# The gate of the state-space mixer: after all token tiles, or tile by tile

## The reference

```
h    = rms_norm(x) ;  proj = h @ w_in            # all three mixers' inputs
A    = sparse attention, B = band attention      # 512 columns each
C    = state-space mixer                         # 1024 columns: 16 heads in 4 groups
x   += concat[A, B, C] @ w_out
x   += relu(rms_norm(x) @ w_up)^2 @ w_down
```

```
y = y + d_skip * xs
g = (y * silu(z)).reshape(b, t, 4, 256)
g = g * rsqrt(mean(g * g, axis=-1) + EPS)        # per token and group
out = g.reshape(b, t, 1024) * gate_norm
```

## Time and profile before

| what | value |
|---|---|
| median of three runs | 3196.65 us |
| the profiled execution | 3198.03 us |
| its span, first to last instruction | 3196.3 us |
| TensorE busy | 3107.2 us, 97% |
| VectorE busy | 1714.7 us, 54% |
| ScalarE busy | 1146.5 us, 36% |
| mean granted TensorE clock | 0.982 |
| rate of all transfers | 139 GB/s over the span |

### The profile page before, as it was taken

How to read it: one execution, slowest core, us unless ns; L and a number is a source line. 1 busy time by engine, 2 the same in 40 slices (tenths; PEclk the granted TensorE clock), 3 DMA queues, 4 the chain that set the end, 5 groups by cost and what they waited for, 6 DMA issues and landing times.

```text
span 3196.3 us, 52626 instructions
## 1 busy us (share of the span) xinstructions
PE 3107.2 (97%) x20829; PEld 3054.1 (96%) x20829; DVE 1714.7 (54%) x2135; ACT 1146.5 (36%) x1373; POOL 136.9 (4%) x115
## 2 busy tenths in 40 slices
PE   6999999899999999999999999998999999999998
PEld 5899999799999999999999999987999999999998
DVE  5574467685435444444555735587654444444444
ACT  3334443243333333233323435433433333332333
POOL 4000000020000000000110000000100000000001
PEclk8999999899999999999999999998999999999999
DMA  6444444244445445454444544422454444544542
GB/s 203 122 139 130 148 139 126 66 125 145 149 148 150 150 147 150 151 147 149 151 124 133 155 140 127 146 94 79 145 151 148 148 151 149 147 150 151 147 148 92
DMA packets 233862, 444.41 MB, mean 139 GB/s; under 512 B 23073, under 2 KB 23521, under 8 KB 233425
## 3 DMA queue, kind: packets, MB, share of 16 engines
q1 hardware_dynamic: 228320, 426.37, 44.2%
q0 software_dynamic: 5424, 16.43, 1.6%
HBM read 430.94 MB, written 12.85 MB: 139 GB/s over the span
## 4 chain that ended last, share of the span: by engine, by line
PE 67%; issue 28%; DVE 2%; DVEq 1%; ACT 1%; POOLq 1%; DMA 0%; ACTq 0%; SPq 0%
PE G L682 21%; PE G L683 20%; PE G L684 20%; PE M L719 1%; PE M L957 1%; PE M L851 1%; PE M L905 1%; POOLq L528 1%; PE M L959 0%; DVEq L1375 0%; PE M L796 0%; PE M L777 0%; DMA U<-in_x_prompt 0%; PE M L710 0%; PE M L963 0%
## 5 line engine op out<-in xcount | busy, mean ns | idle before, releaser
L1347 DVE TENSOR_TENSOR raw_parts<-raw,whi 128x1024 fp32r<-128x1024 f32 (+1 forms) x816 | 1016.5, 1261 | 867.0 <-ACT whi L1078 851.4
L1078 ACT ACTIVATE whi<-raw 128x1024 fp32r<-128x1024 f32 (+1 forms) x816 | 849.8, 1045 | 1425.0 <-PE G L684 1389.9
L682 PE MATMUL G<-X_parts,whi 128*128 128x320 f32 x3840 | 1199.7, 312 | 24.8 <-DVE raw_parts L1347 23.3
L684 PE MATMUL G<-X_parts,raw_parts 128*128 128x320 f32 x3840 | 1188.9, 310 | 0.0
L683 PE MATMUL G<-X_parts,whi 128*128 128x320 f32 x3840 | 1188.6, 310 | 0.0
L682 PE MATMUL G<-U_parts,whi 128*128 128x320 f32 x2560 | 798.4, 312 | 12.3 <-DVE U_parts L1516 12.3
L683 PE MATMUL G<-U_parts,whi 128*128 128x320 f32 x2560 | 793.8, 310 | 0.0
L684 PE MATMUL G<-U_parts,raw_parts 128*128 128x320 f32 x2560 | 793.8, 310 | 0.0
L682 PEld LDWEIGHTS G<-X_parts,whi 128*128 128x128 f32 x3840 | 723.2, 188 | 30.8 <-issue 24.8
L683 PEld LDWEIGHTS G<-X_parts,whi 128*128 128x128 f32 x3840 | 723.3, 188 | 0.4
L684 PEld LDWEIGHTS G<-X_parts,raw_parts 128*128 128x128 f32 x3840 | 722.8, 188 | 0.0
(11 more groups left out here) (269 smaller groups left out, 1354.7 us busy)
## 6 DMA issues: line engine op xcount, KB each, us to landing
raw<-in_w_up SPq DMA_DIRECT2D x256, 512.0 KB, 3.7
raw<-in_w_down SPq DMA_DIRECT2D x256, 512.0 KB, 3.7
raw<-in_w_in SPq DMA_DIRECT2D x224, 512.0 KB, 3.6
raw<-in_w_out SPq DMA_DIRECT2D x64, 512.0 KB, 3.7
U<-in_x_prompt SPq DMA_DIRECT2D x2, 1024.0 KB, 7.6
out_y_prompt<-U SPq DMA_DIRECT2D x8, 256.0 KB, 2.5
bias_ext<-XC POOLq DMA_DIRECT2D x2, 768.0 KB, 5.7
raw<-in_w_in SPq DMA_DIRECT2D x16, 80.0 KB, 2.0
```

Source lines behind the costliest of these rows:

```text
L682: pe.matmul(out, hi, xh, start=(i == 0 and k == 0), stop=False)
L684: mm = pe.matmul(out, lo, xh, start=False, stop=(c == part[1] - 1 and k == KC - 1))
L1078: act.activation(whi[:, c % 4, :, cols], raw[:, c, :, cols], ACT.Copy).then_inc(high_done.sem, 1)
L1347: dve.tensor_tensor(wlo[:, c, :, cols], raw[:, c, :, cols], whi[:, c % 4, :, cols].bitcast(F32), ALU.subtract)\
```

## The change

The gate's work is done by tile of tokens and not by group of columns. The squares of tile t (one instruction over all eight blocks) come on ScalarE after the exponents in group (t+1,0); the sums (`gate_sums`, two matmuls of 4 x n columns, all four groups of columns in one bank) on TensorE after `st` of group (t+1,1); the root on ScalarE in that same group; the reciprocal, its application and the split of the operand on VectorE after `weights` in group (t+1,2). The last tile's follow directly on group (2,3). `x_mix` is raised twice, at the end of the last tile. The list of fillings gets three keys `gs` in place of four, two of them between the groups. The due slot of the gate goes.

```diff
@@ mixer_fills
         keys += [("y", t, g), ("st", t, g)]
+        if t and g == 1:
+            keys.append(("gs", t - 1))
         if g < C_GROUPS - 1:
             continue
+        if t == 2:
+            keys.append(("gs", 2))
...
-    keys += [("gs", g) for g in range(C_GROUPS)]
@@ tensor
+                def gate_sums(t):
+                    o, n = TILES[t]
+                    pe.wait_ge(gsq.sem, gsq.at(l, t + 1))
+                    key = ("gs", t)
+                    free_bank(pe, l, key)
+                    for b in range(2):
+                        mm = pe.matmul(mb(key)[:, 0:C_GROUPS * n].rearrange("p (g t) -> p g t", g=C_GROUPS), ones[:],
+                                       SQZ[:, b:2 * C_GROUPS:2, o:o + n], start=(b == 0), stop=(b == 1))
+                    done_filling(mm, key)
...
+                    if t and g == 1:
+                        gate_sums(t - 1)
                     if g < C_GROUPS - 1:
                         continue
+                    if t == 2:
+                        gate_sums(2)
@@ scalar
+                def gate_squares(t):
+                    o, n = TILES[t]
+                    act.wait_ge(gz.sem, gz.at(l, t + 1))
+                    act.activation(SQZ[:, :, o:o + n], Z[:, :, o:o + n], ACT.Square).then_inc(gsq.sem, 1)
+                def gate_roots(t):
+                    o, n = TILES[t]
+                    key = ("gs", t)
+                    filled(act, l, key)
+                    drained(act.activation(GRMS[:, :, o:o + n], mb(key)[:, 0:C_GROUPS * n].rearrange("p (g t) -> p g t", g=C_GROUPS),
+                                           ACT.Sqrt, scale=1.0 / (C_WIDTH // C_GROUPS), bias=eps[:, 0:1]), key)
+                    act.drain().then_inc(grms.sem, 1)
...
+                    if t and g == 0:
+                        gate_squares(t - 1)
+                    if t and g == 1:
+                        gate_roots(t - 1)
                     if g < C_GROUPS - 1:
                         continue
+                    if t == 2:
+                        gate_squares(2)
+                        gate_roots(2)
@@ vector
+                def gate(t):
+                    o, n = TILES[t]
+                    dve.wait_ge(grms.sem, grms.at(l, t + 1))
+                    dve.reciprocal(GRMS[:, :, o:o + n], GRMS[:, :, o:o + n])
+                    dve.drain()
+                    for kb in range(2 * C_GROUPS):
+                        zb = Z[:, kb, o:o + n]
+                        dve.scalar_tensor_tensor(out=zb, in0=zb, scalar=pcol("gate", kb), in1=GRMS[:, kb // 2, o:o + n],
+                                                 op0=ALU.mult, op1=ALU.mult)
+                    dve.drain()
+                    for j in range(2, 4):
+                        m4 = MIX[:, 4 * j:4 * j + 4, o:o + n]
+                        hi, lo = (U_parts[:, i, 4 * j:4 * j + 4, o:o + n] for i in range(2))
+                        dve.tensor_copy(hi, m4)
+                        dve.drain()
+                        ins = dve.tensor_tensor(lo, m4, hi.bitcast(F32), ALU.subtract)
+                        if t == 2:
+                            ins.then_inc(x_mix.sem, 1)
...
                     gated(t, g)                      # raises gz after g == 3
                     if k + 1 < len(groups):
                         weights(*groups[k + 1])
+                    if t and g == 2:
+                        gate(t - 1)
...
-                dve.drain().then_inc(gz.sem, 1)
-                yield due["gate"]
-                gate()
+                gate(2)
```

More of the change, by code:

```diff
@@ L128, in schedule @@
         due["so", t] = at + 5 * t + 5
-    due["gate"] = at + 17
     return due
@@ L408, in trunk @@
     so_out = Count(nc, "state_rows_stored", 2, step=16)
-    gz = Count(nc, "gated", 1)
-    gsq = Count(nc, "gate_squares", 4)
-    grms = Count(nc, "gate_rms", 4)
+    gz = Count(nc, "gated", 3)
+    gsq = Count(nc, "gate_squares", 3)
+    grms = Count(nc, "gate_rms", 3)
     passed = sem("waits_passed")
@@ L1747, in gated @@
                     dve.tensor_tensor(Z[:, 2 * g:2 * g + 2, o:o + n], Z[:, 2 * g:2 * g + 2, o:o + n], YT[:, :, 0:n], ALU.mult)
+                    if g == C_GROUPS - 1:
+                        dve.drain().then_inc(gz.sem, 1)
                     key = ("st", t, g)
@@ L1758, in gated @@
                     dve.drain().then_inc(st_ready.sem, 1)
[L1760 to L1764, removed]
-                        dve.drain()
[L1766 to L1772, removed]
+                def gate(t):
[12 more added lines that the diff above has]
+                        dve.tensor_copy(hi, m4)
+                        dve.drain()
+                        ins = dve.tensor_tensor(lo, m4, hi.bitcast(F32), ALU.subtract)
+                        if t == 2:
+                            ins.then_inc(x_mix.sem, 1)
                 yield due["cb"]
```

## The result

The changed kernel takes 3241.2 us (median of 4 runs, 3240.0 to 3242.3) against 3194.5 us (3190.2 to 3198.3) for the kernel before on the same chip: ratio 1.0152, 95% interval 1.0139 to 1.0164. It is slower by 46.7 us, where 36 were forecast; 3241.2 lies inside the range of 3210 to 3248. The profiled executions differ by 43.3 us (spans of 3239.6 and 3196.3 us).

What follows compares the result with a forecast made beforehand. TensorE, busy 97% of the span, was taken as the bound. Terms 6.9 + 8.7 + 5.4 - 3.0 = 18.0 us per layer, 36.0 for two, took the profiled 3198.03 to 3234.0 us, stated as 3232.7; range 3210 to 3248.

Steps and rivals of the forecast that it cites:

- step 1: Sums of tile 0 on TensorE wait for VectorE to drain their bank: pause, sums and low clock, 6.9 us per layer.
- step 2: VectorE's gate of tile 0 delays the residual, so TensorE stalls at slot 132: 7.3 us plus 1.4 of clock, 8.7.
- step 3: Sums of tile 1, in tile 2, meet the same bank wait: 5.6 us, of which 5.4 arrive at weights of (2,3).
- step 4: Tail after group (2,3): less gate remains, but tile 1's gate stands before `gated` (2,3); 3.0 us gained per layer.
- The clock: After TensorE pauses the following matmuls run at a low clock: 1.7, 1.4 and 1.4 us, 4.5 per layer.
- A: Neither sums nor gate hold TensorE up; only the tail's 3.0 us gain per layer remains, 3190.6 us; chance 3%.
- B: Bank wait not felt; only the gate of tile 0 stalls the unit, 8.1 us per layer, 3212.9 us; chance 7%.
- C: Bank waits as worked out, but the residual of unit 2 not late: 9.3 us per layer, 3215.3 us; chance 6%.
- D: Each new TensorE pause costs 2.8 us of low clock: 3.9 us more per layer, 3240.5 us; chance 15%.

Runs made afterwards that it cites:

- late_sums: Changed kernel with TensorE's sums and ScalarE's root of tiles 0 and 1 moved from group (t,1) to (t,2), one group later; 3221.9 us, ratio 1.0082.
- gates_last: Changed kernel with VectorE's gate of tiles 0 and 1 moved behind the gated product of group (2,3), ahead of tile 2's; 3232.7 us, ratio 1.0120.
- gate_first_table_clear2: gate_first plus a one-column root preloading ScalarE's table, and GpSimd's clearing (not its store) moved behind the split of the last half; 3182.0 us, ratio 0.9963.
- busy_pauses: Changed kernel with TensorE's pauses ahead of the sums of tiles 0 and 1 filled by 6 and 4 zero matmuls; 3225.4 us, ratio 1.0094.
- two_roots_out: Changed kernel with the square roots of tiles 0 and 1 replaced by a copy, so two table switches per layer instead of six; 3243.3 us, ratio 1.0156.
- late_and_last: Changed kernel with the moves of late_sums and gates_last together; 3223.9 us, ratio 1.0088.
- gate_first_clear2: gate_first with GpSimd's clearing of its sums moved behind the split of the last half, the store left in place; 3190.0 us, ratio 0.9979.
- gate_first: Kernel before with the gated product's semaphore raised right behind the product of (2,3) and TensorE's and ScalarE's gate work ahead of the state rows; 3190.2 us, ratio 0.9990.

## Why the prediction was right, and where its size was off

**The pause ahead of the first sums (step 1).** 3.5 us forecast, 3.44 measured, ended by L1706 as named; the delay of what follows 6.9 and 7.06. Shown by late_sums, where the wait is gone.

**The gate of tile 0 (step 2).** 8.1 us of VectorE forecast, 7.9 measured; the stall at slot 132 7.3 and 6.88; slot 132 late by 14.2 us by the sum (6.9 + 7.3) and by the trace. Shown by gates_last, where the stall is gone.

**The second sums (step 3).** Pause 2.5 and 2.57 us. The delay added from slot 132's chunk to (2,2) was put at 5.4 us; the products of (2,2) come at 639.67 where 618.57 less 2.94, 615.63, would be the undelayed start. That is a delay of 24.0 us, and 16.9 had arrived at the products of (2,1) (625.24, before 611.27): 7.1 us.

**The tail (step 4).** 3.0 us of gain forecast; the delay falls from 24.0 to 21.4, 2.7 us. That the gate of tile 1 would stand in front of `gated` (2,3) is seen at 655.27. On its way are the 0.8 us that the 1.09 us cast lost beside GpSimd's clearing, while its fellow takes 0.29. And gate_first_table_clear2 shows that such a gain needs no tiles: the order of the end gives more of it.

**The clock: the term that was mis-sized.** Steps 1 and 2 counted 1.7 and 1.4 us of low clock, step 3 another 1.4, the tail nothing: 4.5 us per layer. Measured in the first layer are 1.9 (7.06 less 3.44 and 1.72 us for the sums), 2.7 (16.9 less 14.2), 2.8 (7.1 less 2.57 and 1.72) and, after the tail, 20 matmuls of 0.47 us instead of 10, some 1.2: about 8.5 us. That is 4 us more per layer, and 18.0 + 4 = 22.

The traces give 22.6 us for the first layer (21.4 and the 1.2) and 23.5 for the second (22.5 and 8 more matmuls at the low level, 1.0), 46.1 us in all. The two profiled executions differ by 43.3, because the changed kernel came to the stage 2.94 us earlier.

What failed was the size of the clock's terms, in three places. Step 2 read half a chunk where nearly a whole one ran at the low level (21 matmuls of 0.47 us after 600.44). Step 3 counted its sums at the full level; they took 3.75 us, and 1.95 in busy_pauses. The tail was given nothing. busy_pauses is the test of it: with the first and the third pause as long but busy, 7.6 us per layer are gone, though the filling accounts directly for 4.5 of them.

**Rivals.** A, B and C needed one of the three waits to be missing; all are there. D, given 15%, came nearest: its price was 8.4 us of low clock per layer and 3240.5 us. Part of that is luck. It put 2.8 us on each of three pauses, measured are 1.9, 2.7 and 2.8, and the 1.2 us behind the tail, which it did not have, fill the gap. No cost of the table switches shows (two_roots_out).

**How the savings combine.** late_sums and gates_last together bring 17.3 of 27.8 us. The waits of late_sums are shorter by only 12.0 + 2.9 + 1.6 - 8.7 = 7.8 of its 19.3 us. The rest is clock. In the first layer's traces it is at the sums, which now take 1.96 and 1.88 us instead of 3.46 and 3.75, and behind the stall at slot 132 (9 matmuls of 0.47 us instead of 21). What gates_last gains is clock behind the same stall, so the two kernels save in part the same thing: against late_sums, late_and_last has waits that are 5.0 us longer for the two layers, and behind slot 132 only 9 slow matmuls per layer are left for it to save. This is read from the traces; no run tests it by itself.

## What to carry to other kernels

Work that is meant to fill an engine's idle time must not stand in the queue in front of something the busiest engine will wait for, and every instruction put on that busiest engine brings its place in the ring of banks with it: ask who drains the bank four keys back. Price a pause of a few microseconds at its length plus two or three microseconds of lower clock (1.9, 2.7 and 2.8 here, and once nothing). Before cutting a tail into pieces, try its order: raising one semaphore earlier, taking the gate ahead of the rows to be stored, preloading the table and keeping GpSimd off the cast gave 8 us here by the trace (7 to 16 by the interval), where the tiles as they were placed cost 47.

## What the runs showed of the hardware

A cast of VectorE from one buffer to another does not run beside GpSimd's clearing. Three casts of 128x1280, 0.83 us alone, met it: one started 0.71 us ahead of it during the store's issue (2.58 us), one 0.15 us behind its start (1.72 us), one 0.85 us behind (1.02 us). All three ended 0.69 us after the clearing did. The Trainium skill ("SBUF — State Buffer", "Who interferes with whom") says of VectorE's 2-port modes, which a cast can enter, that whichever of the two engines issues first has the shared ports for its whole instruction, and the other stands still. The two casts that started behind the clearing agree.

With the store's issue the traces are less plain. Four times a cast kept its 0.83 us beside it, and the issue ended 0.47 or 0.48 us after the cast, taking 0.95 to 1.52 us instead of 0.90. But in gate_first_clear2 the issue had started 0.21 us ahead of the cast and gave way, while in gate_first it had started 0.18 us ahead and the cast was held. The recorded starts do not show what decides.

Behind idle pauses of 3.44 and 2.57 us the sums took 3.46 and 3.75 us in the first layer of the changed kernel (granted clock 0.86 and 0.75 in the two stretches). Behind pauses filled with zero matmuls they took 1.96 and 1.95 us, the full level, and TensorE was back 7.6 us earlier per layer, though these matmuls compute nothing. An idle pause of 3.44 us left the clock up once in the six profiled layers that have it (gates_last, first layer).
